# A two-layer hybrid decoder step: prompt and sample in programs of their own, with expert steps of one group between the blocks of the other

## The reference

```python
q = (xb @ wq).reshape(TOK_BLOCK, PEER_HEADS, D_KEY)
s1 = jnp.einsum('thd,hkd->thk', q[..., :D_HALF], k1); s2 = ...
v1, i1 = lax.top_k(s1, 16); v2, i2 = lax.top_k(s2, 16)
cand = v1[..., :, None] + v2[..., None, :]
best, sel = lax.top_k(cand, 16)                 # 16 experts of each of 8 heads
gate = jax.nn.softmax(best, axis=-1)
act = gelu(einsum('thk d,td->thk', u_tab[eidx], xb))
y = einsum('thk,thkd->td', gate * act, v_tab[eidx])
```

## Time and profile before

| | |
|---|---|
| median of 3 runs | 3264.99 us |
| the profiled execution | 3268.03 us, its span 3266.3 us |
| mean granted TensorE clock | 0.859 |
| engines' busy share of the span | PE 76%, DVE 46%, POOL 30%, ACT 20% |
| DMA | 859.83 MB, of it 721.47 MB by indirect gathers; mean 263 GB/s |
| the two expert stages | 775 to 1644 us and 2380 to 3238 us |

### The profile page before, as it was taken

The page is one execution under the profiler, slowest core; times in us unless marked ns, Lnnn a source line. Parts: engine busy times, 40 slices in busy tenths (PEclk is TensorE's granted clock), DMA queues, the critical chain, the costliest instruction groups (busy, mean ns, idle before and its releaser), DMA issues. The chain is left out here.

```text
span 3266.3 us, 24414 instructions
## 1 busy us (share of the span) xinstructions
PE 2494.9 (76%) x7841; PEld 1308.8 (40%) x7841; DVE 1504.7 (46%) x3672; ACT 667.9 (20%) x1486; POOL 994.8 (30%) x843
## 2 busy tenths in 40 slices
PE   7887846785777777778789778948957778777776
PEld 2362312453332333333357567825623333333333
DVE  0113222215666666766413351151076767666753
ACT  0213434112212221211110221110121212212211
POOL 0000067102444444444200232100034444444441
PEclk9998967797889988988899785569978989988988
DMA  6434378335999999999823103312279999999994
GB/s 224 149 109 168 142 257 290 125 103 200 395 398 412 395 402 393 417 397 396 321 90 119 58 1 107 99 65 77 90 315 400 418 397 403 409 393 403 419 404 169
DMA packets 219178, 859.83 MB, mean 263 GB/s; under 512 B 16492, under 2 KB 98885, under 8 KB 137110
## 3 DMA queue, kind: packets, MB, share of 16 engines
q0 software_dynamic: 102400, 721.47, 55.3%
q1 hardware_dynamic: 116681, 137.21, 12.6%
HBM read 845.50 MB, written 13.18 MB: 263 GB/s over the span
## 5 line engine op out<-in xcount | busy, mean ns | idle before, releaser
L1879 POOL DMA_INDIRECT exp_uv<-in_peer_uv_dram,expert x640 | 765.2, 1196 | 1363.9 <-PE exp_acc L1910 840.2
L1909 PE MATMUL exp_acc<-exp_uv,exp_diag 128*128 128x512 f32 x1280 | 756.4, 676 | 409.0 <-ACT exp_diag L1926 408.8
L1960 DVE CUSTOM_DVE_ANT_0 exp_uv<-exp_uv,htok 128x1024 f32<-128x1024 f32 x640 | 773.1, 1227 | 513.7 <-DMA exp_uv<-in_peer_uv_dram,expert 504.7
L1910 PE MATMUL exp_acc<-exp_uv,exp_diag 128*128 128x512 f32 x1280 | 712.4, 640 | 0.0
L1909 PEld LDWEIGHTS exp_acc<-exp_uv,exp_diag 128*128 128x128 f32 x1280 | 257.2, 212 | 800.7 <-ACT exp_diag L1926 534.1
L1910 PEld LDWEIGHTS exp_acc<-exp_uv,exp_diag 128*128 128x128 f32 x1280 | 269.2, 210 | 358.7 <-issue 358.7
L1918 ACT ACTIVATE exp_act<-exp_dots 128x4 f32<-128x4 f32 x160 | 32.9, 205 | 1198.3 <-DVE exp_dots L1960 1198.3
L1926 ACT ACTIVATE exp_diag<-ident,exp_w 128x128 f32<-128x128 f32 x640 | 201.7, 386 | 0.0
L503 PE MATMUL ssd_in_ps<-hT,ssd_in_w 128*128 128x320 f32 x640 | 175.0, 437 | 10.4 <-ACT hT L400 10.4
L503 PE MATMUL peer_q_ps<-hT,peer_q_w 128*128 128x320 f32 x512 | 143.9, 445 | 20.8 <-ACT hT L400 20.8
L503 PEld LDWEIGHTS ssd_in_ps<-hT,ssd_in_w 128*128 128x128 f32 x640 | 123.0, 192 | 62.5 <-issue 12.7
(11 more groups left out here) (398 smaller groups left out, 2449.1 us busy)
## 6 DMA issues: line engine op xcount, KB each, us to landing
ada_w<-in_ada_w_dram SPq DMA_DIRECT2D x12, 2048.0 KB, 7.5
attp_w<-in_ada_w_dram SPq DMA_DIRECT2D x12, 2048.0 KB, 7.8
ssd_in_w<-in_ssd_w_in_dram SPq DMA_DIRECT2D x20, 1024.0 KB, 5.0
peer_q_w<-in_peer_wq_dram SPq DMA_DIRECT2D x16, 1024.0 KB, 5.2
ab_in_w<-in_ab_w_in_dram SPq DMA_DIRECT2D x10, 1024.0 KB, 4.8
exp_uv<-in_peer_uv_dram,expert POOLq DMA_INDIRECT x640, 9.3
out_ssm_sample_dram<-state_hd SPq DMA_DIRECT2D x8, 1024.0 KB, 4.5
ssd_out_w<-in_ssd_w_out_dram SPq DMA_DIRECT2D x4, 2048.0 KB, 7.5
```

The costliest lines, as they stand in the source:

```text
L1879: pool.indirect_dma_start(slot(g)[:], None, table, bass.IndirectOffsetOnAxis(ap=experts[:, g:g + 1], axis=0)).then_inc(landing(g)[0], 16)
L1909: pe.matmul(acc[t % 2][0][:], diag[g % (2 * GRP)][:], slot(g)[:, D:D + 512], start=False, stop=False, skip_group_check=True)
L1910: pe.matmul(acc[t % 2][1][:], diag[g % (2 * GRP)][:], slot(g)[:, D + 512:2 * D], start=False, stop=False, skip_group_check=True).then_inc( ...
L1960: dve.tensor_tensor_reduce(slot(g)[:, 0:D], slot(g)[:, 0:D], m.htok[:, t, :], 1.0, 0.0, ALU.mult, ALU.add, dots[:, i % 2, k:k + 1]).then_i ...
```

## The change

The kernel is cut into programs for `PROMPT` and `SAMPLE` from ab_out on (ab_in, pooling and `stage_attend_sample` stay as they are, the last now ahead of the prompt's attention). Each projection weight behind ab_in is loaded twice, once for 256 moving columns and once for 64. The experts of a group are an object `Experts` with a ring of its own size; each of its **steps** (one group of four gathers) puts instructions on POOL, PE, ACT and DVE, and `Beside` spreads a number of steps over the places of a stage of the other token group. What is left over runs in `rest`. The object `Space` hands out SBUF. All weights but the experts' table come packed by the host so that a block is contiguous per partition; keys, conv state and SSD state come transposed; loops are unrolled. The sample's causal convolution moves from POOL to VectorE, and its SSD state update is written anew. The stages in the new order, with the expert steps beside them:

```diff
+class Beside:
+    def __init__(self, m, places, steps):
+        self.x = m.beside
+        self.due = [(k + 1) * steps // places - k * steps // places for k in range(places)] if self.x else [0] * places
+    def pe(self, eng, k):
+        for _ in range(self.due[k]):
+            self.x.pe(eng)
...
+RINGS = (6, 9, 5, 12)
...
 def build(nc, a, upto=99):
...
     stage_setup(nc, m, a)
     stage_ada(nc, m, a, 0)
+    stage_project(nc, m, "ab_in", a["ab_w_in_pk"], ALL, m.hT[:], m.proj[:], norm=...)
     stage_pool(nc, m, a)
+    stage_attend_sample(nc, m, a)
+    stage_project(nc, m, "ab_out_s", a["ab_w_out_pk"], SAMPLE, m.yT[:, :, TP:T], residual=...)
+    s0 = peer_head(nc, m, a, 0, SAMPLE, held)
+
+    s0.begin(RINGS[0])
+    stage_attend_prompt(nc, m, a, steps=10)
+    stage_project(nc, m, "ab_out_p", a["ab_w_out_pk"], PROMPT, m.yT[:, :, 0:TP], residual=..., steps=2)
+    p0 = peer_head(nc, m, a, 0, PROMPT, held, 4, 1)
+    s0.rest()
+    s0.end()
+
+    p0.begin(RINGS[1])
+    mixer_ssd(nc, m, a, SAMPLE, held, (22, 5, 6, 12, 3, 5))
+    s1 = peer_head(nc, m, a, 1, SAMPLE, held, 5, 2)
+    p0.rest()
+    p0.end()
+
+    s1.begin(RINGS[2])
+    mixer_ssd(nc, m, a, PROMPT, held, (6, 2, 4, 0, 1, 2))
+    p1 = peer_head(nc, m, a, 1, PROMPT, held, 2, 0)
+    s1.rest()
+    s1.end()
+
+    p1.begin(RINGS[3])
+    stage_norm_out(nc, m, SAMPLE)
+    stage_out(nc, m, a, SAMPLE)
+    p1.rest()
+    p1.end()
+    stage_norm_out(nc, m, PROMPT)
+    stage_out(nc, m, a, PROMPT)
```

`mixer_ssd` takes its numbers of steps for ssd_in, conv, scan, state, gate and ssd_out in that order, `peer_head` for peer_q and scores. The steps of one token group:

```diff
+    def pool(self, pool):
+        i = self.i_pool
...
+        lo = 0 if i == 0 else (i - 1) * GRP + self.ring
+        for g in range(lo, min(i * GRP + self.ring, self.n_all)):
...
+            if g >= self.ring:
+                pool.wait_ge(self.mixed, g - self.ring + 1)
+            pool.indirect_dma_start(self.slot(g)[:], None, table, ...)
+    def pe(self, pe):
...
+            for k in range(GRP):
+                g = (i - 1) * GRP + k
+                pe.wait_ge(self.diagd, g + 1)
+                for j in range(2):
+                    ins = pe.matmul(self.acc[j][:], self.diag[g % (2 * GRP)][:], self.slot(g)[:, D + j * 512:D + (j + 1) * 512], ...)
+                ins.then_inc(self.mixed, 1)
+    def act(self, act):
...
+        if self.ring < 2 * GRP and i:
+            self.spread(act, i - 1)
+        if i < self.groups:
...
+            act.wait_ge(self.dotted, (i + 1) * GRP)
+            act.activation(self.act4[:, i % 2, :], self.dots[:, i % 2, :], ACT.Gelu).then_inc(self.acted, 1)
+        if self.ring >= 2 * GRP and i:
+            self.spread(act, i - 1)
+    def dve(self, dve):
...
+        if self.ring < 2 * GRP and i:
+            self.weigh(dve, i - 1)
+        if i < self.groups:
+            for k in range(GRP):
...
+                dve.wait_ge(sem, there)
+                dve.tensor_tensor_reduce(self.slot(g)[:, 0:D], self.slot(g)[:, 0:D], self.htok[:, t, :], ...)
+        if self.ring >= 2 * GRP and i:
+            self.weigh(dve, i - 1)
```

In a projection a step stands ahead of each block on PE, ACT and DVE, while POOL issues all gathers of the stage without a place:

```diff
             def _(pe):
...
+                for i in range(blocks):
+                    by.pe(pe, i)
+                    pe.wait_ge(loaded[i % 2], i // 2 * 16 + 16)
+                    if i >= 2:
+                        pe.wait_ge(taken, (i - 1) * per)
+                    for j in range(per):
+                        for c in range(kcn):
+                            ins = pe.matmul(at(i, j), wt[i % 2][:, c, j * P:(j + 1) * P], src[:, c, :], ...)
```

The adaLN rows go to four strips of 32 partitions, which a second multiplication sums; each state of the SSD update stays in one buffer from load to store:

```diff
         for c in range(KC):
-            ins = pe.matmul(bank[0:NCOND, :], self.m.cT[:, c, :], self.wt[k][:, c, :], start=(c == 0), stop=(c == KC - 1))
+            o = QUAD * (c % 4)
+            ins = pe.matmul(bank[o:o + QUAD, :], self.m.cT[:, c, :], self.wt[k][:, c, :], start=(c < 4), stop=(c >= 4))
...
+                for b in range(NSEQ):
+                    by.pe(pe, b)
+                    pe.wait_ge(loaded[b % 2], 16 * (b // 2 + 1))
+                    for g in range(SG):
+                        ins = pe.matmul(psO[g][0:TS, :], m.cz[:, g, b * TS:(b + 1) * TS], hb[b % 2][:, g * 512:(g + 1) * 512], ...)
...
+                        pe.matmul(psN[g % 2][:], bm[b % 2][:, g * NST:(g + 1) * NST], m.xes[:, g * 512:(g + 1) * 512], ...)
```

More of the change, by code:

```diff
@@ L337, in _ @@
             def _(sp):
-                with sp.Fori(0, Ada.STEPS) as i:
+                for i in range(Ada.STEPS):
                     for k in range(2):
@@ L343, in _ @@
             def _(pe):
-                with pe.Fori(0, Ada.STEPS) as i:
+                for i in range(Ada.STEPS):
                     for k in range(2):
@@ L351, in _ @@
             def _(act):
-                with act.Fori(0, Ada.STEPS) as i:
+                for i in range(Ada.STEPS):
                     for k in range(2):
@@ L357, in _ @@
             def _(dve):
-                with dve.Fori(0, Ada.STEPS) as i:
+                for i in range(Ada.STEPS):
                     for k in range(2):
@@ L465, in stage_project @@
+def stage_project(nc, m, name, w, part, src, out=None, kcn=KC, bw=256, residual=None, norm=None, after=None, conv=None, steps=0):
+    n, per, blocks = part.n, bw // P, w.shape[0]
+    x = m.xT[:, :, part.cols]
+    wide = per * n > 512
+    with Stage(nc, m, name) as s:
+        wt = [s.sb(f"w{i}", [P, kcn, bw]) for i in range(2)]
         tmp = s.sb("part", [P, TS])
-        ps = [[s.bank(f"ps{i}{j}") for j in range(2)] for i in range(2)]
+        ps = [[s.bank(f"ps{i}{j}") for j in range(per if wide else 1)] for i in range(2)]
@@ L467, in stage_project, with at @@
         loaded = [s.sem(f"w_loaded{i}") for i in range(2)]
-        made = [s.sem(f"made{i}", opened=True) for i in range(2)]
-        taken = [s.sem(f"taken{i}", opened=True) for i in range(2)]
+        made = s.sem("made")
+        taken = s.sem("taken")
         vecd = s.sem("tmp_ready")
-        norm = norm and Norm(s, m, *norm)
         tapped = s.sem("tap_added")
+        if norm:
+            norm = Norm(s, m, part, *norm)
+        by = Beside(m, blocks, steps)
+        def at(i, j):
+            return ps[i % 2][j][:, 0:n] if wide else ps[i % 2][0][:, j * n:(j + 1) * n]
@@ L1674, in stage_scores @@
         hkept = s.sem("h_kept")
-        cleared = s.sem("qz_cleared")
+        by = Beside(m, 1, steps)
+        sets = [(t, g) for t in range(1 if sample else 2) for g in range(2 if sample else 4)]
+        rows = [(t, g) for t in range(1 if sample else 2) for g in range(2)]
         with nc.Block() as block:
@@ new lines, in stage_norm_out, with _, stage_out @@
+def stage_norm_out(nc, m, part):
+    with Stage(nc, m, f"norm_out_{part.name}") as s:
+        norm = Norm(s, m, part, m.vcol[:, 128:136], None)
+        with nc.Block() as block:
+            @block.scalar
+            def _(act):
+                norm.scalar(act)
+            @block.tensor
+            def _(pe):
+                norm.sum(pe)
+            @block.vector
+            def _(dve):
+                norm.vector(dve)
+def stage_out(nc, m, a, part):
+    with Stage(nc, m, f"out_{part.name}") as s:
+        rows = s.sb("rows", [P, len(part.tiles), D])
@@ L2012, in stage_out @@
         stored = s.sem("stored")
+        jobs = [(i, t, g) for i, t in enumerate(part.tiles) for g in range(2)]
         with nc.Block() as block:
```

1689 lines of the change are left out of this document (917 added, 772 removed).

## The result

The changed kernel takes 3855.99 us (median of 4 runs, 3853.76 to 3859.0) against 3271.2 (3261.94 to 3280.45): 1.179 times as long, 95% interval 1.175 to 1.183. I had forecast 3520 and a range up to 3720: the sign was right; 255 us more was forecast and 585 more was measured.

| stretch | forecast | measured |
|---|---|---|
| start to the sample's first experts | 519 | 548 |
| sample experts beside the prompt's attention | 454 | 500 |
| prompt experts beside the sample's SSD | 1180 | 1341 |
| sample experts beside the prompt's SSD | 634 | 698 |
| last experts | 710 | 744 |

The account below looks back on a forecast made before the run. Half the kernel was taken as gather-bound, the rest as bound by PE or chains between engines. Terms 519 + 454 + 1180 + 634 + 710 + 26 = 3523, stated as 3520 us, 8% slower; range 3250 to 3720.

Parts of the forecast that it names:

- start to the sample's first experts: Opening stretch: setup to sample's attention 352, adaLN 72, ab_out 21, peer_q 47, scores 27; 519 us.
- sample experts beside the prompt's attention: Ring of 6: ten steps of 13 us each add themselves whole to the attention, 258; stretch 454 us.
- prompt experts beside the sample's SSD: Ring of 9, the deciding stretch: 64 turns of 16 us, 1024, plus 156 not covered; 1180 us.
- sample experts beside the prompt's SSD: Ring of 5: three gathers land inside a step, 15.4 us in a chain, 8 in a projection; stretch 634 us.
- last experts: End of the kernel: sample's norm and output 18, then 64 groups at 10.5 with start and end, 692; 710 us.
- the signs that I had named: First SSD stretch: restarts every 15 to 17 us, DMA share near 0.7, dot and diagonal waits; last experts 10.5, adaLN near 72.
- with PE at half clock in a third of the turns ... 16: Prompt experts beside the sample's SSD: turn of 15.3 us becomes 16 when PE is at half clock in a third.
- colder and more crowded: Rival: PE at half level in each turn, third gather issued at 8.7, turn 19.2 us, near 3790; chance 0.11.
- about 0.22 each: Sample's programs: a multiplication of 64 columns takes about 0.22 us, against 0.53 for 320 columns.
- The split: Projections done twice: 768 weight tiles multiplied twice, 169 us more and 82 less.
- Overlap works: Rival: the turn falls to what DMA and PE need, 3071 us; chance 0.15, whole or nearly.
- a point of 12.5 us a turn: Prompt experts beside the sample's SSD: below a turn of about 12.5 us the change is no loss.

Follow-up runs that it names:

- the run with 256 columns: Changed kernel with its own order and rings, the sample's ssd_in multiplying 256 columns where it multiplied 64: 3850 us, 1.177 times the kernel before.
- the run without 18 of these loads: Changed kernel, but the sample's ssd_in loads only its first two weight blocks and uses them for all 20: 3861 us, 1.181 times the kernel before.
- the serial run: Changed kernel with no expert step beside any stage, each of four expert groups alone with a ring of 12: 3572 us, 1.092 times the kernel before.
- Undone in a serial kernel: Serial version of the changed kernel with the five projections run once on all 320 columns: 3291 us, 1.005 times the kernel before.
- with the weights first: Changed kernel, ring of 9 kept, old group's weights put before the new group's dots beside the sample's SSD: 3511 us, 1.075 times the kernel before.
- the steps beside the sample's SSD alone: Changed kernel, weights first at ring 9; the sample's two expert groups run alone with a ring of 12: 3399 us, 1.041 times the kernel before.

## Why the prediction was wrong in size

The mechanism, a turn made of issue, landing and dot, was right, and its terms were too small. In all 331 us are missing, 161 of them in one stretch. Of the signs that I had named, the DMA share near 0.7 and the waits at the dots and diagonals came; the turns of 15 to 17 us, the last experts at 10.5 a group and adaLN near 72 did not.

*Prompt experts beside the sample's SSD (+161).* The step that failed is "with PE at half clock in a third of the turns ... 16". PE begins the mixing at half clock, the lower level, in 62 of the 63 turns, after 4.9 us of idle time in the one shown. So the third issue is at 8.6 and not at 7.1 (6.4, and 8.7 in a third of the turns); and the third gather lands 8.4 us later, not 7.7. Together a turn is 18.2 and not 16, and 64 x 2.2 = 141 of the 161, by these terms 96 from the clock and 45 from the landing. The turns that ran warm in the run with 256 columns bear it out: 6.3 for the third issue and 16.4 in all. It was my rival "colder and more crowded" (8.7 + 9.3 + 1.2 = 19.2), of which the colder half was right. Of the other half, the landing is longer than I said but not by the weight loads, since it is 8.4 in the mean without them too. The estimate of 68 us from the Trainium skill's rule that DMA engines go round between queues (DMA: Bandwidth & Descriptors, Queues, rings and completion order) shows in no time here, since the run without 18 of these loads is as slow. That I gave the rival 0.11 was the error of judgement: the earlier trace rows shows a group that began at half clock even where nothing but DMA held PE up, and my own text said that PE would idle for 5 us in each turn.

*Start (+29).* Two narrow projections came to 34 and 64 us instead of 21 and 47, by the term "about 0.22 each", from the earlier trace rows. Those eight multiplications stood right behind the wide ones of a mixing, as do the 3.68 us for 16 in the timeline above; a stage made of nothing else gets 0.43. The row was the right operation in the wrong surroundings. AdaLN came to 83 us, not 72: DMA share 0.78, not over 0.9. Scores (18 us, not 27) and the sample's attention (3 less) gave 12 back.

*Sample experts beside the attention (+46).* Ten steps at 19.7 us ((318 - 121) / 10, with the attention of the serial run) and not 13. Where the mixing begins at half clock, the second gather is let go 7.6 us after the weights, not 4.6; a step with its dots is then 14.4 (602.7 to 617.1 in the timeline). The ten of them come to 147 us together; the choice of the next experts, which I had not counted, adds some 20 (3.9 of them from 617.1 to 621.0), and the first step waits 14 for its first gathers. The other 16 were not traced. The stage without steps was 121, 7 less than I said, and ab_out, peer_q and scores together 14 less.

*Sample experts beside the prompt's SSD (+64).* Scan and gate of the prompt alone are 84 and 49 us in the serial run, where I had 69 and 28 by proportion, and 4 steps in the scan are 94 us, not 62. I had also read the stages outside the experts as 12 GB/s and more; one row has 0, which changes no term.

*Last experts (+34).* Turns of 10.78 in the mean, not 10.5 (63 x 0.28 = 18), and 16 more at the start and end.

*The split.* I put 87 us on it net (169 - 82). Undone in a serial kernel it is 282. In the changed kernel itself much of that seems to be hidden behind the turns, and so it did little to the error; that is read from the sum and not from a run. The best interleaving tried gains 173 us on the serial kernel, less than the 282, and so stays above the kernel before.

*Overlap works*, the rival on the other side, I had tied to a point of 12.5 us a turn, below which the change is no loss. That point was wrong too: with the weights first the turn beside ssd_in is 12.6 and the prompt's experts take about 1000 us, near the 924 to 988 I gave for turns of 12 to 13, and the kernel takes 3511, not 3227 to 3291. The start, the two sample groups and the last experts, 173 us over my terms in the changed kernel, are still in it. The gain is real but smaller than the 282 us that the split costs. The Trainium skill's rule (Perfetto Trace Analysis, Identifying Performance Opportunities) that interleaving regimes may help is borne out by the steps beside the sample's SSD alone against serial, 173 us; with steps in all three places it is 62 us in the one order (3511) and a loss of 284 in the other (3856). In these runs what decides is not how idle the other resource is, but whether the ring holds two groups *and* the order leaves a gather a whole turn to land. I had counted the slots and taken the order as given; the cheap remedy I did not see.

## What to carry to other kernels

Before two regimes are interleaved, write down for the loop that moves into the gaps what must be freed, issued and landed between two of its steps: if that is anything of the same step, its latency is paid each time, and changing the order of two instructions can be worth more than slots. Price a narrow multiplication by a row that stands among its like, not by one behind wide work. Splitting a small batch from a large one loads every weight tile twice, which here cost 282 us before any overlap could pay. And a break-even taken for one stretch holds only if the other stretches keep their price.

## What the runs showed of the hardware

A stage of 64-column multiplications, each with weights of its own, keeps PE busy for 96% of its time and is granted 0.50 throughout (140.47 of 146 us). The Trainium skill (TensorE: Matmul & The Clock Gate, What's actually happening) says that the clock follows how busy the engine has been of late; here PE was busy by the profile and stayed at the lower level, and the measurement decides. With 256 columns in the same place the clock is 0.97, and the time is the same (141.44 us busy). The Trainium skill (TensorE: Matmul & The Clock Gate, HAM oscillation) advises padding for thin products whose loop waits for DMA; this stage hardly waits, and padding to 256 columns restored the clock and gained nothing (3587 against 3572 us).

Eighteen loads of 1 MB taken out beside gathers, at a DMA share of 0.73, left the stage as long as it was, though these loads took 8.2 us to land in the median where they took 5.0 before. What they lengthened was the landing of the fourth gather in a row, 10.9 us for 8.9.

A gather of 1.05 MB issued with none in flight ahead of it landed after 5.5 us in the median, the next one after 7.4 and the third after 8.3 (the 20 turns of the changed kernel beside ssd_in, issues 1.7 us apart).
